# A long convolution's filter spectrum from quarters of the taps, with the products of the transform in another order

## What is computed

```python
def _hyena_filter(L, w1, b1, fr1, w2, b2, fr2, w3):
    ...
    h = jnp.sin(fr1 * (feats @ w1 + b1))
    h = jnp.sin(fr2 * (h @ w2 + b2))
    h = (h @ w3) * jnp.exp(-t * deltas[None, :])
    h_f, h_b = h[:, :HY_WIDTH], h[:, HY_WIDTH:]
    kern = jnp.concatenate([h_f, zeros, h_b[1:][::-1]], axis=0)
    return kern / (jnp.sum(jnp.abs(kern), axis=0, keepdims=True) + EPS)

def _long_conv(u, kern):
    uf, kf = jnp.fft.rfft(u, n=2 * L), jnp.fft.rfft(kern, n=2 * L)
    return jnp.fft.irfft(uf * kf)[:, :L]
```

## Time and profile before

| | |
|---|---|
| median of 3 runs | 946.96 us (946.65 to 947.83) |
| the profiled execution | 948.66 us; span 946.6 us |
| TensorE matmul busy | 922.2 us, 5602 instructions |
| VectorE busy | 619.2 us, 808 instructions |
| ScalarE busy | 348.0 us, 605 instructions |
| GpSimd busy | 26.9 us, 36 instructions |
| TensorE's granted clock, mean over the span | 0.996 |

### The profile page before, as it was taken

One profiled execution on the slowest core, in us unless ns is written; L12 is line 12 of the kernel. 1 busy time (PEld: TensorE's weight loads), 2 busy tenths in 40 slices (PEclk: granted clock), 3 DMA queues, 4 the chain that ended last, 5 costly groups with the idle time before them and its releaser, 6 DMA issues.

```text
span 946.6 us, 13811 instructions
## 1 busy us (share of the span) xinstructions
PE 922.2 (97%) x5602; PEld 822.7 (87%) x5602; DVE 619.2 (65%) x808; ACT 348.0 (37%) x605; POOL 26.9 (3%) x36
## 2 busy tenths in 40 slices
PE   8999999999999999998999999999999999999996
PEld 4479898898898888687889999889999988999985
DVE  5754666957858856897677766446666634566656
ACT  5754433333333333232654433212333421234333
POOL 2200000100000000001000000000000000000000
PEclk9999999999999999999999999999999999999999
DMA  9664323423422353319021222222222222122102
GB/s 313 207 223 153 115 86 134 125 83 121 153 95 90 135 171 81 122 21 246 0 90 67 90 90 68 89 90 67 69 67 90 68 89 84 56 85 68 45 1 111
DMA packets 34342, 98.31 MB, mean 104 GB/s; under 512 B 3767, under 2 KB 11959, under 8 KB 33640
## 3 DMA queue, kind: packets, MB, share of 16 engines
q1 hardware_dynamic: 30920, 86.63, 27.8%
q0 software_dynamic: 3040, 10.78, 4.3%
q10 hardware_dynamic: 320, 0.04, 0.0%
HBM read 94.27 MB, written 3.16 MB: 103 GB/s over the span
## 4 chain that ended last, share of the span: by engine, by line
PE 76%; DVE 15%; ACT 4%; issue 3%; DMA 2%; ACTq 0%; SPq 0%; DVEq 0%
PE ps L1582 21%; PE ps L1584 21%; PE ps L1583 21%; PE ps L1803 3%; PE ps L1602 2%; DVE w_lo L1080 2%; DMA raw<-in_slots 1%; DVE o_hg L1308 1%; PE ps L1815 1%; PE ps L1663 1%; PE ps L1940 1%; ACT w_hi L727 1%; PE ps L1625 1%; DMA w<-in_hy_w 1%; PE ps L1823 1%
## 5 line engine op out<-in xcount | busy, mean ns | idle before, releaser
L1582 PE MATMUL ps<-h_hi,w_hi 128*128 128x320 f32 x1152 | 360.7, 313 | 2.7 <-DVE w_lo L1080 1.4
L1584 PE MATMUL ps<-h_hi,w_lo 128*128 128x320 f32 x1152 | 355.9, 309 | 0.0
L1583 PE MATMUL ps<-h_lo,w_hi 128*128 128x320 f32 x1152 | 355.9, 309 | 0.0
L1582 PEld LDWEIGHTS ps<-h_hi,w_hi 128*128 128x128 f32 x1152 | 216.5, 188 | 4.0 <-issue 2.3
L1583 PEld LDWEIGHTS ps<-h_lo,w_hi 128*128 128x128 f32 x1152 | 216.5, 188 | 0.1
L1584 PEld LDWEIGHTS ps<-h_hi,w_lo 128*128 128x128 f32 x1152 | 216.3, 188 | 0.0
L1080 DVE TENSOR_TENSOR w_lo<-raw,w_hi 128x1024 fp32r<-128x1024 f32 x106 | 129.4, 1225 | 110.4 <-ACT w_hi L727 106.8
L727 ACT ACTIVATE w_hi<-raw 128x1024 fp32r<-128x1024 f32 x106 | 110.8, 1052 | 95.0 <-PE ps L1584 91.6
L1583 PE MATMUL ps<-w_lo,a_hi 128*128 128x512 f32 x220 | 85.6, 389 | 0.0
L1582 PE MATMUL ps<-w_hi,a_hi 128*128 128x512 f32 x220 | 85.6, 389 | 0.0
L1584 PE MATMUL ps<-w_hi,a_lo 128*128 128x512 f32 x220 | 85.6, 389 | 0.0
(11 more groups left out here) (279 smaller groups left out, 1020.0 us busy)
## 6 DMA issues: line engine op xcount, KB each, us to landing
raw<-in_slots SPq DMA_DIRECT2D x138, 512.0 KB, 3.8
raw<-in_slots SPq DMA_DIRECT2D x24, 256.0 KB, 5.8
xin<-in_x_sample SPq DMA_DIRECT2D x4, 512.0 KB, 10.8
grow<-gates POOLq DMA_DIRECT2D x2, 1024.0 KB, 12.8
x<-in_x_sample POOLq DMA_DIRECT2D x2, 1024.0 KB, 13.3
out_y_sample<-x SPq DMA_DIRECT2D x4, 512.0 KB, 3.1
ktab<-in_ktab POOLq DMA_DIRECT2D x1, 1024.0 KB, 9.0
lead_hi<-in_slots SPq DMA_DIRECT2D x4, 256.0 KB, 11.3
```

Source lines behind the costliest of these rows:

```text
L1582: mm(out, lhs[0], rhs[0], start=first, stop=False)
L1583: mm(out, lhs[0], rhs[1], start=False, stop=False)
L1584: return mm(out, lhs[1], rhs[0], start=False, stop=last)
```

## The change

The taps of the latent filter are ordered in four quarters, by the residue of the position by 4 (0, 2, 1, 3), and the second frequency block is the first one mirrored. Then the even taps' sum and difference need products with one block's table alone: `even_dft` makes quarter 0 and quarter 2 in two banks (two matmuls for one cs), ScalarE copies the second of them out (`take_second`), and VectorE's `even_part` adds and subtracts them into `kspec` for both blocks. `odd_dft` makes the odd taps' sum of one block and one cs (two matmuls) in a bank that the even part has left, and `join` adds and subtracts that, reading the odd sum directly from the bank. So there are four even and eight odd products for sixteen, two copies by ScalarE for four, and on VectorE four operations of `even_part` and eight of `join` for eight of `join`. The table `ktab` has ten blocks of 128 for sixteen (640 KB for 1024 KB).

In the order of the work: on TensorE both even parts and the first two odd groups stand ahead of the turns of x, the other two odd groups behind quad 1. On ScalarE the copies stand between squares 3 and 4 and behind square 4, ahead of the root. On VectorE `even_part(0)` stands ahead of the inverse, `even_part(1)` ahead of `join(0)`; `join(2)` stands with `join(3)` behind `tap_size(3)`. On POOL's queue `ident` is issued ahead of `rates`, and `rates` waits for `hcol` and w2.

```diff
--- before.py
+++ after.py
@@ -256,6 +256,10 @@
 TAP_ORDER = (2, 0, 3, 1, 4)
 
 
+RESIDUES = (0, 2, 1, 3)
+KTAB = [(_f, _i) for _f in ("cos", "sin") for _i in range(4)] + [("-cos", 3), ("-sin", 3)]
+
+
 def constants():
 
     c = {}
@@ -272,7 +276,8 @@
         ang = (np.float32(2.0 * math.pi) * pos[:, None].astype(np.float32) * bands[None, :] / np.float32(L)).astype(np.float32)
         return t, np.concatenate([t[:, None], np.cos(ang), np.sin(ang)], 1)
 
-    ts, fs = feats(TS, order)
+    quarters = np.concatenate([np.arange(r, TS, 4) for r in RESIDUES])
+    ts, fs = feats(TS, quarters)
     tp, fp = feats(TP, np.arange(TP))
     f = np.concatenate([fs, fp]).T.astype(np.float32).reshape(NEMB, NT, P)
     c["feats"] = np.ascontiguousarray(f[:, list(SIDES[0] + SIDES[1])].reshape(NEMB, 2 * SIDE))
@@ -288,16 +293,19 @@
 
 
 
-    th = math.pi * (2 * np.arange(TS // 2) + 1) / (2 * TS)
+    rising = np.arange(P)
+    th = math.pi * (2 * np.concatenate([rising, TS // 2 - 1 - rising]) + 1) / (2 * TS)
     n = order.reshape(2, 2, P)
 
-    def tab(shift):
-        a = n[..., None] * th if not shift else (n[..., None] + 0.5) * th
+    def tab():
+        a = (n[..., None] + 0.5) * th
         return np.stack([np.cos(a), np.sin(a)], 0)
 
-    c["ktab"] = np.ascontiguousarray(tab(0).transpose(3, 0, 1, 2, 4).astype(np.float32))
-    c["utab"] = np.ascontiguousarray(tab(1).transpose(3, 0, 1, 2, 4).astype(np.float32))
-    inv = tab(1).reshape(2, 2, 2 * P, 2, P) / TS
+    quarter = quarters.reshape(4, P)[..., None] * th[:P]
+    wave = {"cos": np.cos(quarter), "sin": np.sin(quarter), "-cos": -np.cos(quarter), "-sin": -np.sin(quarter)}
+    c["ktab"] = np.ascontiguousarray(np.stack([wave[f][i] for f, i in KTAB], 1).astype(np.float32))
+    c["utab"] = np.ascontiguousarray(tab().transpose(3, 0, 1, 2, 4).astype(np.float32))
+    inv = tab().reshape(2, 2, 2 * P, 2, P) / TS
     c["itab"] = np.ascontiguousarray(inv.transpose(4, 3, 0, 1, 2).astype(np.float32))
     tg = math.pi * (2 * np.arange(TP) + 1) / (2 * TP)
     m = np.arange(TP)
@@ -380,7 +388,7 @@
         decay = sb(early, "decay", [NT, HW])
         filt = sb(early, "filt", [2, NT, HW])
         size = sb(early, "size", [2, HW])
-        ktab = sb(early, "ktab", [2, 2, 2, 2 * P])
+        ktab = sb(early, "ktab", [len(KTAB), P])
         ptab_k = sb(early, "ptab_k", [2, TP])
         row_e = sb(early, "row_e", [HW])
         part = sb(early, "part", [2, HW])
@@ -544,7 +552,11 @@
         def spectrum(n):
 
 
-            return 1 - n // 2, 1 - n % 2
+            return 1 - n % 2, 1 - n // 2
+
+        def odd_bank(n):
+
+            return (6, 7, 4, 5)[n]
 
         def score_bank(h, j):
 
@@ -651,10 +663,12 @@
                                   allow_slow_non_contiguous=True).then_inc(sem("gate_out"), 16)
 
             load(vec[:, :], io["vec"], "ld_vec")
+            load(ident[:, :], io["ident"], "ld_ident")
+            eng.wait_ge(sem("ld_hcol"), 32)
+            eng.wait_ge(sem("ld_hid"), 32)
             load(rates, io["rates"], "ld_rates")
-            load(ident[:, :], io["ident"], "ld_ident")
             eng.wait_ge(sem("raw_in0"), 32)
-            load(ktab[:, :, :, :, :], io["ktab"], "ld_ktab")
+            load(ktab[:, :, :], io["ktab"], "ld_ktab")
             load(ptab_k[:, :, :], io["ptab"][:, 0], "ld_ktab")
 
 
@@ -795,13 +809,11 @@
                 eng.wait_ge(sem("x_inverse"), 1)
                 A(xin[:, i, :], xin[:, i, :], ACT.Copy, scale=stat[:, 0, 1, i:i + 1]).then_inc(sem("x_scaled"), 1)
 
-            def take_odd(n):
-
-                cs = spectrum(n)[1]
+            def take_second(n):
+
+                cs = 1 - n
                 eng.wait_ge(sem("kdft"), n + 1)
-                if n >= 2:
-                    eng.wait_ge(sem("kspec_ready"), n - 1)
-                A(part[:, cs, :], ps[:, 4 + 2 * cs + 1, :], ACT.Copy).then_inc(sem("kodd"), 1)
+                A(part[:, cs, :], ps[:, 4 + 2 * cs + 1, :], ACT.Copy).then_inc(sem("second_taken"), 1)
 
             def tap_abs(n):
 
@@ -814,24 +826,23 @@
 
             square_x(0)
             ada_row(0)
-            for i in range(1, NT):
+            for i in range(1, 4):
                 square_x(i)
+            take_second(0)
+            square_x(4)
+            take_second(1)
             eng.wait_ge(sem("x_squared"), NT)
             A(stat[:, 0, 1, :], stat[:, 0, 0, :], ACT.Sqrt, scale=1.0 / D, bias=eps[:, :]).then_inc(sem("x_rooted"), 1)
             for i in range(2, NT):
                 scale_x(i)
-            take_odd(0)
-            take_odd(1)
             split_hi(0)
             modulate(0)
             modulate(1)
-            take_odd(2)
             tap_abs(0)
             tap_abs(1)
             tap_abs(2)
             ada_row(1)
             tap_abs(3)
-            take_odd(3)
             tap_abs(4)
             split_hi(1)
             modulate(2)
@@ -1184,11 +1195,20 @@
             def join(n):
 
                 m, cs = spectrum(n)
-                eng.wait_ge(sem("kodd"), n + 1)
-                even = ps[:, 4 + 2 * cs, :]
-                link(V.tensor_tensor(kspec[:, m, 0, cs, :], even, part[:, cs, :], ALU.add))
-                first, second = (even, part[:, 0, :]) if cs == 0 else (part[:, 1, :], even)
-                link(V.tensor_tensor(kspec[:, m, 1, cs, :], first, second, ALU.subtract), "kspec_ready")
+                eng.wait_ge(sem("kdft"), n + 3)
+                even, odd = kspec[:, m, 0, cs, :], ps[:, odd_bank(n), :]
+                first, second = (even, odd) if cs == 0 else (odd, even)
+                link(V.tensor_tensor(kspec[:, m, 1, cs, :], first, second, ALU.subtract))
+                link(V.tensor_tensor(even, even, odd, ALU.add), "kspec_ready")
+
+            def even_part(n):
+
+
+                cs = 1 - n
+                eng.wait_ge(sem("second_taken"), n + 1)
+                both = (ps[:, 4 + 2 * cs, :], part[:, cs, :])
+                link(V.tensor_tensor(kspec[:, 0, 0, cs, :], *both, ALU.add))
+                link(V.tensor_tensor(kspec[:, 1, 0, cs, :], *(both if cs == 0 else both[::-1]), ALU.subtract), "even_ready")
 
             eng.wait_ge(sem("silu_exp"), 1)
             link(V.tensor_scalar(gate_c, gate_c, 1.0, None, ALU.add))
@@ -1199,6 +1219,7 @@
                 damp(n)
             sum_groups(0)
             gain_pair(0)
+            even_part(0)
             eng.wait_ge(sem("x_rooted"), 1)
             link(V.reciprocal(stat[:, 0, 1, :], stat[:, 0, 1, :]), "x_inverse")
             scale_x(0)
@@ -1209,20 +1230,21 @@
 
             link(V.tensor_tensor(bound[:, 3, :], bound[:, 2, :], bound[:, 2, :], ALU.subtract))
             link(V.tensor_scalar(bound[:, 4, :], bound[:, 3, :], -1.0, 1.0, ALU.mult, ALU.add))
+            even_part(1)
             join(0)
             join(1)
             split_lo(0)
             split_h(0)
             split_h(1)
-            join(2)
             tap_size(0)
             tap_size(1)
             sum_groups(1)
             gain_pair(1)
             tap_size(2)
             tap_size(3)
+            join(2)
             join(3)
-            eng.wait_ge(sem("kdft"), 5)
+            eng.wait_ge(sem("kdft"), 7)
             link(V.tensor_copy(kspec_p[:, :, :], ps[:, 6:8, :]), "kspec_ready")
             tap_size(4)
             split_lo(1)
@@ -1650,19 +1672,28 @@
                                                ident[0:2 * GROUP, 0:2 * GROUP])
                 last.then_inc(sem("sums_turned"), 1)
 
-            def filter_dft(n):
-
-
-                m, cs = spectrum(n)
+            def wave(f, i):
+                return ktab[:, KTAB.index((f, i)), :]
+
+            def even_dft(n):
+
+
+                cs = 1 - n
                 eng.wait_ge(sem("taps_ready"), 4)
                 eng.wait_ge(sem("first_row"), 1)
-                if n >= 2:
-                    eng.wait_ge(sem("kspec_ready"), n - 1)
-                for e in range(2):
-                    for k in range(2):
-                        last = mm(ps[:, 4 + 2 * cs + e, :], ktab[:, cs, e, k, m * P:(m + 1) * P], filt[:, cs, 2 * e + k, :],
-                                  start=(k == 0), stop=(k == 1))
+                for i in range(2):
+                    last = mm(ps[:, 4 + 2 * cs + i, :], wave(("cos", "sin")[cs], i), filt[:, cs, i, :], start=True, stop=True)
                 last.then_inc(sem("kdft"), 1)
+
+            def odd_dft(n):
+
+
+
+                m, cs = spectrum(n)
+                eng.wait_ge(sem("even_ready"), n // 2 + 1)
+                f = ("cos", "sin")[cs ^ m]
+                mm(ps[:, odd_bank(n), :], wave(f, 2), filt[:, cs, 2, :], start=True, stop=False)
+                mm(ps[:, odd_bank(n), :], wave("-" * m + f, 3), filt[:, cs, 3, :], start=False, stop=True).then_inc(sem("kdft"), 1)
 
             def turn_prompt(k):
 
@@ -1704,9 +1735,11 @@
             eng.wait_ge(sem("ld_ident"), 16)
             ada_turn(0)
             eng.wait_ge(sem("ld_ktab"), 32)
-            filter_dft(0)
+            even_dft(0)
```

(10 more changed lines are left out.)

## The result

The changed kernel took 949.95 us in the median of its runs, the kernel before 947.83 in the runs beside it: ratio 1.0027, interval 1.0015 to 1.0039. One of its 15 executions took 1833.1 us and is left out of the ratio; nothing on record shows why. So it was slower by 2.1 us and by 1.3; forecast was +1.2, counted as "no change", with slower at 0.19. The profiled execution took 949.03 us, a span of 947.2.

The account below looks back on a forecast made before the run. It took VectorE's fourth join, which TensorE's turn of column group 2 awaits, as the bound. Fourth join 0.5 us sooner and +1.7 for a half-clock stretch gave +1.2 us: 948.2 from a median of 946.96, range 945.0 to 950.0.

Parts of the forecast that it names:

- Products: Transform on TensorE: twelve products for sixteen, 3.6 us less work and a 0.76 us wait gone, becoming waiting for VectorE.
- Start, w2: Start: with rates moved behind w2, the hidden layer starts at about 7.6 in place of 8.52, -0.9 us.
- Start, rates: Start, POOL's queue: rates issued at about 7.6, landing at 12.5 before ScalarE needs it at 13.0, cost nil.
- a rival at 0.06: Start: rates takes ktab's 9.0 us, landing at 16.6, total about 951; or w2 no sooner, 949.1. Chance 0.06.
- ScalarE's copies, +1.0: ScalarE, among the squares: two copies ahead of the root make root, inverse and scaling 1.0 us later.
- VectorE to the fourth join, 17.2 + 0.95: VectorE from the inverse: 17.2 us of work without idle, plus 0.95 for an addition held by POOL's add; join at 44.15.
- Pause and clock: TensorE ahead of column group 2's turn: some 4 us waiting, then one stretch at half clock, +1.7 us.
- The rival with two stretches: Pause ahead of column group 2's turn: clock low for two stretches, price 3.4 - 0.5 = +2.9, total 949.9. Chance 0.17.
- Sum: Whole kernel: -0.5 for the sooner fourth join and +1.7 for the clock make +1.2 us, 948.2 on the median.
- VectorE's joins are the bound: Stretch up to the fourth join: VectorE's joins keep TensorE's gain from arriving; the rival, whole gain, 942.6, had chance 0.05.

Follow-up runs that it names:

- e11: Kernel before with only the change's move of rates (GpSimd's queue, behind the wait for b1 and w2), old transform: 948.41 us, ratio 1.0009.
- e7: Kernel before with only the load of rates moved to ScalarE's queue behind w2, old transform: 946.81 us, ratio 0.9999.
- e4: Changed kernel with rates issued on ScalarE's queue right behind w2, without a wait: 947.29 us, ratio 0.9988 to the kernel before.
- e2: Changed kernel with the third join directly behind the second tap size on VectorE, ahead of the small addition: 947.98 us, ratio 1.0009 to the kernel before.
- e1: Changed kernel with sixteen small throwaway products keeping TensorE at work in its pause: 947.44 us, ratio 0.9998 to the kernel before.
- e6: Changed kernel with the edits of e1, e2 and e4 together: 946.51 us, ratio 0.9983 to the kernel before.
- e10: e8 with two tap sizes put ahead of the copy of the prompt's spectrum on VectorE: 944.11 us, ratio 0.9961 to the kernel before.
- e9: Old transform with the order of e10, rates on ScalarE's queue included: 946.11 us, ratio 0.9994 to the kernel before.
- e5: The changed kernel run again, unaltered, in a later comparison: 948.96 us, ratio 1.0011 to the kernel before.
- e8: Changed kernel with rates as in e4, VectorE's joins ahead of the tap sizes, tap sums later: 942.36 us, ratio 0.9950 to the kernel before.
- e13: e10 with rates issued later on ScalarE's queue, behind the hidden layer's first sine: 943.59 us, ratio 0.9971 to the kernel before.
- e12: e10 with rates left where the change has them, on GpSimd's queue behind w2: 946.28 us, ratio 0.9988 to the kernel before.

## Why the prediction was wrong, point by point

- **Products.** Right: the first value tile was done at 40.5 (39.9 forecast, which counted on an inverse 0.64 sooner), and the gain became a wait.
- **Start, w2.** Right: the hidden layer's products at 7.72, 0.8 sooner for 0.9 forecast.
- **Start, rates: the step that failed.** I took "today's 4.9 us" from the earlier trace rows and added it to an issue at 7.6: landed 12.5, "cost nil". It was issued at 7.71 to 8.13 in six profiles and took 6.3 to 7.7 us: landed at 14.02 to 15.81, where 13.0 was wanted. The row of 4.9 us was taken at 1.94; SP issued the pieces of the ring only from 5.08 on. I had a row of the later time, ktab's 9.0, and used it only in a rival at 0.06. What the start gave in place of 0.9 is shown by e11, the old transform with rates landed at 14.38: 0.12 us at the inverse. So this term was 0.78 off, and more in the executions with the inverse at 27.73 and 28.02.
- **ScalarE's copies, +1.0.** Nearly right. e11 and the changed kernel have rates at about the same time (14.38 and 14.44), and ScalarE waits for nothing from there to the root; the inverse is at 25.77 with the old transform and at 26.64 with the copies, 0.87 later. ScalarE's timeline of e11, then of the changed kernel:

```profile
24.20 1.04 ACT L793 ACTIVATE kspec_p<-xin 128x1024 f32<-128x1024 f32 x1
...
25.36 0.30 ACT L822 ACTIVATE stat<-stat,eps 128x5 f32<-128x5 f32 x1
```

```profile
24.25 0.58 ACT L816 ACTIVATE part<-ps 128x512 f32<-128x512 f32 x1
24.73 1.05 ACT L805 ACTIVATE kspec_p<-xin 128x1024 f32<-128x1024 f32 x1
...
26.24 0.29 ACT L835 ACTIVATE stat<-stat,eps 128x5 f32<-128x5 f32 x1
```

  With rates in time the copies cost only 0.17 (inverse 24.82 in e7, 24.99 in e4): without them ScalarE waits among the squares, for the quad and for the last tile of x (landed at 23.22 in e7, its square at 23.24), so that from the first square to the root it takes 6.57 us in e7 for 5.80 in e11. The copies fill most of these waits.
- **VectorE to the fourth join, 17.2 + 0.95.** Right: 18.24 without idle, 17.29 without the hold (e2).
- **Pause and clock.** Right in place and in kind: 4.44 us of waiting, one stretch at 0.50 of 3.41 us, 1.4 us lost for 1.7. (Two stretches cost 2.6 in e4, from the fourth join's end at 43.22 to the next value tile at 49.87 against the 4.06 of e1; forecast was 3.4.) The Trainium skill, "TensorE: Matmul & The Clock Gate", section "Why this matters for your kernels", warns of such gaps between bursts; this trace agrees, and e1 and e6, with the gap filled, show no fall there. The rival with two stretches came in two of four profiles that kept the pause of 4.4 us (4.44 and 4.45 one stretch, 4.43 twice two), so 0.17 looks low for it, as far as four profiles tell.
- **Sum.** The fourth join came 0.21 later than before, not 0.5 sooner; with 1.4 for the clock that is +1.6 at the next value tile (50.36 for 48.73), and +3.8 in the execution with later rates and two stretches (52.55). The medians' 2.1 and 1.3 suit a mixture of such executions, which is argued and not shown. That +1.6 lies near the +1.2 of the sum is in part luck: the start was 0.78 worse, the copies 0.13 and the clock 0.3 better than forecast. The median, 949.95, fell inside my range by 0.05; the change was slower where I had said no change.
- **"VectorE's joins are the bound"** was right, and e10 beside e9 shows it: the same transform gains 3.3 us once they stand first.

## What to carry to other kernels

Work taken off an engine gives time only where that engine ends the stretch; where another does, it turns into a pause, and on TensorE the pause was paid a second time here, in the clock (1.4 us for one stretch at half). So move the waiting engine's order with it: here, at the first projection and with rates in time, the new transform alone was 2.25 us later (e4 for e7), the new order alone 0.49 sooner (e9 for e7), both together 3.83 sooner (e10 for e7). And price a moved transfer by what lands at its new hour, not by its own duration at the old one.

## What the runs showed of the hardware that I had not expected

**Run times lie in two groups, by the granted clock.** Beside e5 to e8 the kernel before ran 29 times: 15 executions with a mean granted clock of 0.996 or 0.997 took 946.09 us in the median, 13 at 0.993 or 0.994 took 949.30. The changed kernel's 11 there all lay at 0.993 to 0.995, its stretch ahead of the first projection among them. e10 and e13 reach the first projection at 62.52 and 62.56, yet their spans are 942.8 and 939.3: the late clock was at half once for 6.83 us and once for 3.41. The same sums ahead of it start 0.22 us apart (427.62 and 427.40), the same turns behind it 3.46 (463.45 and 459.99). Windows of e10, then of e13:

```profile
439.83:446.66 6.83, 6.83 (x22) 5.78 (x22) 2.98 (x6) 0.30 (x1) 0.00 (x0) 0.50 0.18 72
```

```profile
430.47:433.88 3.41, 3.41 (x13) 3.02 (x13) 3.23 (x7) 1.27 (x3) 0.00 (x0) 0.50 1.11 246
```

So a median also tells how many executions fell in each group. Of e10's twelve, five lie at 0.996 or 0.997 (median 941.50) and seven at 0.994 (944.58); all five of e8 lie at 0.995 to 0.997, so its lower median doesn't show a better order. Group by group (executions at 0.995 left out), e9 (945.16 and 948.10) lies 3.7 and 3.5 above e10, and e12 (943.91, of two, and 946.86) 2.4 and 2.3: the transform in this order is worth 3.5 us or so, and the place of rates what the first projection says.

**VectorE waits out GpSimd's additions, but not in every operation.** The addition of 128x8 beside GpSimd's 128x512 ends when that one does (1.13 us for 0.17, 0.90 in e10). Nor is it only small operations: in e10 a tap size of 0.69 us that began inside an addition of GpSimd's took 1.66. VectorE's line, then GpSimd's:

```profile
43.52 1.66 DVE L1180 TENSOR_TENSOR decay<-decay 128x512 f32<-128x512 f32 x1
```

```profile
42.84 1.79 POOL L688 TENSOR_TENSOR feats<-feats,decay 128x512 f32<-128x512 f32 x1 [1.33 <-DVE decay L1180]
```

In the changed kernel a tap size that began at 41.30, just ahead of GpSimd's addition at 41.35, kept its 0.69, and that addition took 1.77 in place of 1.29. The four operations of the joins from 42.03 on, which read one operand from a bank, kept their 0.69 beside GpSimd (41.35 to 44.53). So in these profiles the operation that began later was the longer, and operations with an operand in a bank were spared; no run here shows the reason.
